# Last expert group by column halves, a one-pass second norm carried over the border, and thin norms in the second block

## The chip, the cores and the metric
The kernel runs on one core of one Trainium2 chip. The metric is the device time in microseconds from launch to end. TensorE (PE) multiplies, with its weight loads (PEld) beside it; VectorE (DVE), ScalarE (ACT) and GpSimd (POOL) work on tiles; SyncE (SP) issues the DMAs. All data is fp32.

## The reference
Two transformer blocks run one after the other, each of two layers, on 256 tokens of width 1024 (the first block adds 16 meta tokens, so T = 272 columns there). What matters here:

```
for l in range(2):                                   # first block
    mix = concat(deltanet(h), sparse_attention(h)) @ w_out[l]
    h = layer_norm(ALPHA * h + mix, ln1_g[l], ln1_b[l])
    ffn = hier_moe(h, ...)                           # 32 experts, top 2 of one group
    h = layer_norm(ALPHA * h + ffn, ln2_g[l], ln2_b[l])
layer_norm(x) = (x - mean) * rsqrt(var + 1e-5) * g + b
rms_norm(x)   = x * rsqrt(mean(x * x) + 1e-6) * g
for l in range(2):                                   # second block
    n = rms_norm(h, ln_mix[l]); mem = rms_norm(memory, mem_norm[l])
    p = n @ w_in[l]        # q, k, v, gates, ..., glow (16 columns), merge gates
    h = h + (gated sum of three branches: sparse, gated linear, memory) @ w_out[l]
    h = h + relu(rms_norm(h, ln_mlp[l]) @ w_up[l]) ** 2 @ w_down[l]
```

## The kernel before
The residual hT stays in SBUF, transposed: 8 tiles of 128 features by T tokens. A mean over features is a matmul with mean_w, a 128x128 matrix of 1/1024, summed over the eight tiles in PSUM, so each norm has 8 such products (and a layer norm 8 for the mean and 8 for the variance). In the trace one fp32 matmul leaves two records.

**Experts** (`experts`, L1409). Tokens are packed into groups of four blocks of 32 slots. For each group TensorE gathers the rows (L1401, e_sel), multiplies with w1 (L1531, x = 0) and w3 (x = 1), transposes (L1539), projects down in two banks (`down`, L1549, e_Wd), and `scatter` (L1510) spreads the result of the group before over the tokens with the gates `e_back`; VectorE adds each part to hT (L1685). Weights come over one queue, SyncE's: w1, w3 and Wd of a group are four DMAs of 1 MB each. ScalarE makes silu and copies y (L1628). A loop runs over the groups (n is read from a table); the last group follows it: turn, scatter of the group before, down, scatter of the last, its adds (L1750), and then `layer_norm_steps` (L1079): mean (L1087), subtraction (L1112), squares (L1100), variance (L1094), logarithm and exponential for the root (L1102, L1104), scale (L1115), shift (L1107). Then come the block's end, `clear` (semaphores set to zero on all engines and a barrier, L1774) and the next block of code. In layer 1 `turn_memory` (L1559) also transposes the memory tokens, ScalarE copies and squares them (L1649, L1650), and L1602 sums their squares.

**Second block** (`products`, L2118). It issues all products of w_in and w_out. Each engine's order comes from merging several streams (products, heads, sparse, gated, memory) by planned times: `F.start(key)` and `F.end(key)` come from a table of product lengths through the curve TIMES2, and the chains have fixed times. The order of products is mk (memory keys, 4), mv (memory values, 2), glow, kw, vwg (2), gqk, q and so on; two banks alternate, and ScalarE copies most results (L2292). The norm's squares are L2303, its mean square L2172, its root L2308 and L2310, its scale L2383 (`p_done`); the memory norm is L2298, L2300 and L2378. In the MLP (`mlp2`) the mean square is L3209, after the second product of 128 columns.

## Time and profile before
| | us |
|---|---|
| median of 3 runs (lowest, highest) | 2337.35 (2334.98, 2340.13) |
| the profiled execution, own time | 2336.61 |
| its span | 2334.7 |
| TensorE busy | 2144.6 |
| VectorE, ScalarE busy | 799.9, 512.2 |
| HBM read | 407.54 MB, 175 GB/s over the span |

The page gives busy time by engine; the gaps of TensorE have to be looked up in the timeline. Its stages: first block, layer 0, to 554; layer 1 to 1087; second block, branches of layer 0 to 1486 and MLP to 1713; layer 1 to the end.

### The profile page before, as it was taken

How to read it: one execution, taken by the hardware profiler on the slowest of the kernel's cores; microseconds unless marked ns; L12 is line 12 of the kernel's file. 1: busy time of each engine (PE TensorE's matmuls, PEld its weight loads, DVE VectorE, ACT ScalarE, POOL GpSimd, SP SyncE). 2: the span in 40 equal slices, each digit the busy share in tenths (PEclk: the TensorE clock that was granted, in tenths of full speed). 3: DMA queues.
4: the chain of work that ended last, by engine and by line, in shares of the span. 5: the costliest groups of instructions: out<-in, count | busy, mean ns of one | idle time of the engine just before them, and what ended most of it. 6: DMA issues, size and time to landing. Idle time of an engine off the chain costs nothing. (4 is left out here: it accounts for less than half of the span.)

```text
span 2334.7 us, 34572 instructions
## 1 busy us (share of the span) xinstructions
PE 2144.6 (92%) x13364; PEld 1646.9 (71%) x13364; DVE 799.9 (34%) x1944; ACT 512.2 (22%) x1187; POOL 64.6 (3%) x84
## 2 busy tenths in 40 slices
PE   7999989778998989778989999999999899999998
PEld 6777766445777766445757777888878577788887
DVE  3464153234465244223253323111124533221112
ACT  2313331003323431004224311100022252201000
POOL 0230000000230000000000000000000000000000
PEclk9989999999999999999999999999999999999999
DMA  6321569994321469996540434334444314343341
GB/s 219 98 91 38 228 273 386 426 424 146 122 92 38 171 276 388 424 425 226 144 153 21 161 91 129 142 144 157 166 106 144 108 67 150 109 149 139 144 144 54
DMA packets 155376, 415.22 MB, mean 178 GB/s; under 512 B 36210, under 2 KB 49756, under 8 KB 130668
## 3 DMA queue, kind: packets, MB, share of 16 engines
q1 hardware_dynamic: 155244, 413.42, 47.9%
q8 instruction: 87, 1.43, 0.2%
q14 instruction: 45, 0.37, 0.0%
HBM read 407.54 MB, written 1.05 MB: 175 GB/s over the span
## 5 line engine op out<-in xcount | busy, mean ns | idle before, releaser
L2200 PE MATMUL bank<-hT,W 128*128 128x256 f32 (+1 forms) x1440 | 328.0, 383 | 6.9 <-ACT b_gates L2350 5.9
L2200 PEld LDWEIGHTS bank<-hT,W 128*128 128x128 f32 (+1 forms) x1440 | 268.5, 190 | 53.8 <-issue 13.6
L265 PE MATMUL bank<-hT,W 128*128 128x272 f32 (+1 forms) x1056 | 262.5, 405 | 14.8 <-PEq L1774 7.6
L265 PEld LDWEIGHTS bank<-hT,W 128*128 128x128 f32 (+1 forms) x1056 | 203.0, 195 | 64.6 <-issue 18.8
L3204 PE MATMUL bank<-hT,W 128*128 128x256 f32 x1024 | 223.6, 379 | 0.0
L3220 PE MATMUL bank<-u_hid,W 128*128 128x256 f32 x1024 | 223.3, 379 | 0.0
L3204 PEld LDWEIGHTS bank<-hT,W 128*128 128x128 f32 x1024 | 194.6, 190 | 27.3 <-issue 1.0
L3220 PEld LDWEIGHTS bank<-u_hid,W 128*128 128x128 f32 x1024 | 194.6, 190 | 26.5
L1531 PE MATMUL bank<-W,e_hs 128*32 128x256 f32 x1664 | 106.9, 417 | 40.8 <-DMA W<-in_w 38.3
L1531 PEld LDWEIGHTS bank<-W,e_hs 128*32 128x32 f32 x1664 | 58.1, 120 | 91.5 <-DMA W<-in_w 44.0
L3280 DVE TENSOR_TENSOR hT<-hT,bank 128x256 f32<-128x256 f32 x128 | 53.9, 421 | 166.5 <-PE bank L3220 166.5
L3249 ACT ACTIVATE u_hid<-u_rel 128x256 f32<-128x256 f32 x64 | 26.6, 416 | 343.8 <-DVEq L3274 343.8
L1510 PE MATMUL bank<-e_back,e_y 128*128 128x272 f32 x288 | 84.5, 415 | 16.3 <-DVE hT L1685 12.2
L1401 PEld LDWEIGHTS bank<-e_sel,rowsH 128*128 128x128 f32 x768 | 92.1, 201 | 8.5 <-issue 5.3
L1401 PE MATMUL bank<-e_sel,rowsH 128*128 128x128 f32 x768 | 95.7, 287 | 1.3 <-DVEq L1729 1.3
L3272 DVE SCALAR_TENSOR_TENSOR u_rel<-bank,rstd 128x256 f32<-128x256 f32 x64 | 27.2, 425 | 203.5 <-PE bank L3204 175.9
L1510 PEld LDWEIGHTS bank<-e_back,e_y 128*128 128x128 f32 x288 | 45.6, 188 | 50.1 <-DVE hT L1685 40.3
L1549 PE MATMUL bank<-e_Wd,e_hidT 128*32 128x512 f32 x512 | 61.1, 620 | 7.7 <-DMA e_Wd<-in_w 6.6
L1194 PE MATMUL bank<-mixT,W 128*128 128x272 f32 x256 | 61.1, 393 | 2.3 <-PEq L1057 2.3
L1685 DVE TENSOR_TENSOR hT<-hT,bank 128x272 f32<-128x272 f32 x128 | 54.5, 436 | 23.3 <-PE bank L1510 19.5
L1690 DVE TENSOR_TENSOR e_hid<-e_sil,bank 128x256 f32<-128x256 f32 x16 | 9.7, 609 | 151.6 <-PE bank L1531 149.8
L1628 ACT ACTIVATE e_y<-bank 128x512 f32<-128x512 f32 x32 | 17.4, 595 | 201.4 <-PE bank L1549 187.0
(570 smaller groups left out, 2674.6 us busy)
## 6 DMA issues: line engine op xcount, KB each, us to landing
W<-in_w SPq DMA_DIRECT2D x104, 1024.0 KB, 16.7
W<-in_w_in SPq DMA_DIRECT2D x38, 2048.0 KB, 8.6
e_Wd<-in_w SPq DMA_DIRECT2D x64, 1024.0 KB, 14.2
W<-in_w_up SPq DMA_DIRECT2D x16, 2048.0 KB, 8.8
W<-in_w_down SPq DMA_DIRECT2D x16, 2048.0 KB, 7.7
e_w_ahead<-in_w SPq DMA_DIRECT2D x20, 1024.0 KB, 13.4
W<-in_w_out SPq DMA_DIRECT2D x8, 2048.0 KB, 8.2
W<-in_mem_w_kv SPq DMA_DIRECT2D x4, 2048.0 KB, 12.2
```

The costliest lines, as they stand in the source:

```text
L265: mm = nc.tensor.matmul(bank[0:rows, 0:T], w[:, k, c0:c0 + rows], m.hT[:, k, :], start=(k == 0), stop=(k == KT - 1))
L1194: mm = nc.tensor.matmul(ps[n % 4][:, 0:T], w[:, k, n % 4 * P:n % 4 * P + P], m.mixT[:, k, :], start=(k == 0), stop=(k == KT - 1))
L1401: mm = nc.tensor.matmul(o, m.rowsH[:, c, d * P:(d + 1) * P], m.sel[:, c, :], start=(c == 0), stop=(c == 2))
L1510: nc.tensor.matmul(ps[6 + d % 2][:, 0:T], y[:, d * P:(d + 1) * P], back[:, 0, :], start=True, stop=True).then_inc(S["e_part"], 1)
L1531: mm = nc.tensor.matmul(ps[2 + x][32 * j:32 * j + 32, DE * x:DE * x + DE], hs[:, k, 32 * j:32 * j + 32], weights, start=(k == 0), stop=(k ...
L1549: mm = nc.tensor.matmul(ps[4 + h][32 * j:32 * j + 32, :], hidT[:, f, 32 * j:32 * j + 32], Wd[:, j, f * D + 512 * h:f * D + 512 * h + 512], ...
L1685: nc.vector.tensor_tensor(m.hT[:, d, :], m.hT[:, d, :], ps[6 + d % 2][:, 0:T], ALU.add).then_inc(S["e_y_free"], 1)
L2200: mm = nc.tensor.matmul(o[0:n, 0:S2], w[:, k, a:a + n], m.hT[:, k, :], start=(k == 0), stop=(k == KT - 1))
L3204: mm = nc.tensor.matmul(ps[j][:, 0:S2], w[:, k, j * P:(j + 1) * P], m.hT[:, k, :], start=(k == 0), stop=(k == KT - 1))
L3220: mm = nc.tensor.matmul(ps[4 + n % 2][:, 0:S2], w[:, k, n * P:(n + 1) * P], hid[:, x, k, :], start=(k == 0), stop=(k == 3))
L3272: nc.vector.scalar_tensor_tensor(rel[:, j, :], ps[j][:, 0:S2], 0.0, m.rstd[:, :], ALU.max, ALU.mult)
L3280: nc.vector.tensor_tensor(m.xT[:, n, :], m.xT[:, n, :], ps[4 + n % 2][:, 0:S2], ALU.add).then_inc(S["u_y_free"], 1)
```

## The change
1. Experts, last group: the loop ends one group earlier. w1 of the last group, then the scatter of the group before, then w3. Wd is loaded in two halves of 512 columns, four DMAs each, on two signals. `down` is called for one half at a time; the eight last scatters use four banks and stand between and behind the halves.
2. The second layer norm is computed in one pass: the mean from the column total of hT (added up on VectorE) plus the mean of y (ScalarE's accumulator) spread by the gates; the variance from squares of the uncentred hT less the squared mean. Squares are added in pairs before the product. hT less the mean is written before the border; root, scale and shift (`norm_end`) are done behind it, in the next layer's mixers (products wait tile by tile for `n2_done`) or in the second block's start. The semaphores of the experts are cleared by GpSimd in the next mixers in layer 0, and by `clear` after layer 1.
3. Memory transpositions use two banks in turn, behind two of the norm's sums.
4. Second block and MLP: the eight squares are added on VectorE (4, 2 and 1 tiles) and one product makes the mean square, behind mk1 in both layers.
5. glow comes with vwg (168 columns instead of 152) and is transposed out of it; mv0 goes ahead of vwg, mv1 behind.

```diff
@@ projections: on_tensor, on_scalar, on_vector, on_gpsimd
                 for k in range(KT):
+                    if l and n == 0:
+                        pe.wait_ge(S["n2_done"], k + 1)
                     mm = nc.tensor.matmul(bank[0:rows, 0:T], w[:, k, c0:c0 + rows], m.hT[:, k, :], start=(k == 0), stop=(k == KT - 1))
...
+        if l:
+            yield -1.0
+            end_on_act(act)
...
+        if l:
+            yield -1.0
+            end_on_dve(dve)
+            dve.wait_ge(S["n2_done"], KT)
...
+        if l:
+            for name in EXPERTS1:
+                pool.sem_clear(S[name])
@@ new
+def norm_end(nc, m, rstd, scaled, done):
+    def on_scalar(act):
+        nc.scalar.activation(m.core.n2_rstd[:, :], m.ps[3][:, 0:T], ACT.Ln, bias=m.eps5[:, 0:1])
+        act.drain()
+        nc.scalar.activation(m.core.n2_rstd[:, :], m.core.n2_rstd[:, :], ACT.Exp, scale=-0.5).then_inc(rstd, 1)
+        for k in range(KT):
+            act.wait_ge(scaled, k + 1)
+            nc.scalar.activation(m.core.hT[:, k, :], m.core.hT[:, k, :], ACT.Identity, bias=m.core.prmT[:, 73 + k:74 + k]).then_inc(done, 1)
+    def on_vector(dve):
+        dve.wait_ge(rstd, 1)
+        for k in range(KT):
+            nc.vector.scalar_tensor_tensor(m.core.hT[:, k, :], m.core.hT[:, k, :], m.core.prmT[:, 65 + k:66 + k], m.core.n2_rstd[:, :], ALU.mult, ALU.mult).then_inc(scaled, 1)
@@ experts: SyncE
-                down(last, n + 1)
+                sp.wait_ge(S["e_down"], n + 1)
+                for h, signal in enumerate((S["e_down_in"], S["e_w3_ahead"])):
+                    for j in range(G):
+                        sp.dma_start(Wd[:, j, :].rearrange("p (f d) -> p f d", f=2)[:, :, 512 * h:512 * h + 512],
+                                     expert_weights(A, l, last[j])[2].rearrange("p (f d) -> p f d", f=2)[:, :, 512 * h:512 * h + 512]).then_inc(signal, 16)
@@ experts: TensorE
+                between(n)
+                up(n + 1, n * 64, only=(0,))
+                scatter(n + 1)
+                up(n + 1, n * 64, only=(1,))
                 turn(n + 1)
-                scatter(n + 1)
-                down(n + 1)
+                pe.wait_ge(S["n2_sums"], SUMS["total"])
+                nc.tensor.matmul(ps[2][:, 0:T], m.mean_w[:, :], total[:, 0, :], start=True, stop=False)
+                down(n + 1, halves=(0,))
+                pe.wait_ge(S["e_back"], n + 3)
+                last_scatter(0, n + 2)
+                last_scatter(1, n + 2)
+                pe.wait_ge(S["e_w3_ahead"], 64 + 64)
+                down(n + 1, halves=(1,))
+                last_scatter(2, n + 2)
+                last_scatter(3, n + 2)
+                pe.wait_ge(S["n2_sums"], SUMS["y"])
+                nc.tensor.matmul(ps[2][:, 0:T], y_mean, back[:, 0, :], start=False, stop=True).then_inc(S["n2_mean"], 1)
...
@@ experts: VectorE
+                nc.vector.tensor_tensor(total[:, :, :], m.hT[:, 0:4, :], m.hT[:, 4:8, :], ALU.add)
+                dve.drain()
+                nc.vector.tensor_tensor(total[:, 0:2, :], total[:, 0:2, :], total[:, 2:4, :], ALU.add)
+                dve.drain()
+                nc.vector.tensor_tensor(total[:, 0, :], total[:, 0, :], total[:, 1, :], ALU.add)
+                dve.drain().then_inc(S["n2_sums"], 1)
+                product(n + 1)
                 turned(n + 1)
...
+                for k in range(KT):
+                    dve.wait_ge(S["n2_squares"], k + 1)
+                    nc.vector.tensor_tensor(m.hT[:, k, :], m.hT[:, k, :], mean, ALU.subtract)
@@ Products: planned lengths
+        add(("mv", 0), 7.0, "act")
         for j in range(2):
-            add(("mv", j), 7.0, "act")
-        add("glow", 3.6, "act")
+            add(("vwg", j), 2.6, "act")
+        add(("mv", 1), 7.0, "act")
+        add("glow", 0.4, "act")
         add("kw", 3.65, "act")
-        for j in range(2):
-            add(("vwg", j), 2.4, "act")
@@ products: TensorE
-            for k in range(KT):
-                pe.wait_ge(S["p_sq"], k + 1)
-                mm = nc.tensor.matmul(ps[6][:, 0:S2], m.mean_w[:, :], m.hT[:, k, :], start=(k == 0), stop=(k == KT - 1))
-            mm.then_inc(S["p_ms"], 1)
-        if l:
-            mean_square()
+            pe.wait_ge(S["p_sum"], 1)
+            nc.tensor.matmul(ps[6][:, 0:S2], m.mean_w[:, :], m.hT[:, 0, :], start=True, stop=True).then_inc(S["p_ms"], 1)
...
+        for c in range(2):
+            mm = nc.tensor.transpose(o[0:16, c * P:(c + 1) * P], m.vwg[:, c, 152:168], m.ident[:, :])
@@ products: ScalarE, first layer
+            nc.scalar.activation(m.core.n2_rstd[:, :], m.core.n2_rstd[:, :], ACT.Exp, scale=-0.5).then_inc(S["x_rstd"], 1)
+            for k in range(KT):
+                act.wait_ge(S["x_scaled"], k + 1)
+                nc.scalar.activation(m.core.hT[:, k, :], m.core.hT[:, k, :], ACT.Identity, bias=m.core.prmT[:, 73 + k:74 + k])
+            act.drain()
+            copy(("mk", 0), m.kT[:, 0, :])
@@ products: VectorE (the MLP does the same with u_squares)
+            dve.wait_ge(S["p_sq"], KT)
+            for half in (4, 2, 1):
+                nc.vector.tensor_tensor(m.hT[:, 0:half, :], m.hT[:, 0:half, :], m.hT[:, half:2 * half, :], ALU.add)
+                dve.drain()
+            dve.drain().then_inc(S["p_sum"], 1)
```

What this makes of the order, in the words of the built programs. TensorE, end of layer 0, before (the eight single scatters L1510 of each run shown once; hT, e_y, e_back are the residual, the result, the gates):

```order
L1531 MATMUL bank<-W,e_hs 32x256 x32
...
L1539 MATMUL bank<-k_ident,e_hid 128x128 x2
...
L1510 MATMUL bank<-e_back,e_y 128x272
...
L1549 MATMUL bank<-e_Wd,e_hidT 32x512 x16
...
L1087 MATMUL bank<-hT,k_mean_w 128x272 x8
L1094 MATMUL bank<-mixT,k_mean_w 128x272 x8
L1448 UNCONDITIONAL_BRANCH
L1773 ISA x6
```

The same place in the changed program (L1549 is the scatter there, L1609 a last scatter, L1590 the down projection, L1614 a sum for the norm):

```order
L1572 MATMUL bank<-W,e_hs 32x256 x32
...
L1549 MATMUL bank<-e_back,e_y 128x272
...
L1572 MATMUL bank<-W,e_hs 32x256 x32
L1580 MATMUL bank<-k_ident,e_hid 128x128 x2
L1649 MATMUL bank<-e_w_ahead,k_mean_w 128x272
...
L1590 MATMUL bank<-e_Wd,e_hidT 32x512 x8
...
L1609 MATMUL bank<-e_back,e_y 128x272
...
L1590 MATMUL bank<-e_Wd,e_hidT 32x512 x8
...
L1614 MATMUL bank<-mixT,k_mean_w 128x272
```

The scatter of the group before stands ahead of w3, and the down projection is in two pieces with scatters between them; the 16 products of the norm are seven, among the scatters. ScalarE behind the border to layer 1, changed program:

```order
L1730 ACTIVATE mixT<-hT 128x272 x8
L1483 UNCONDITIONAL_BRANCH
L1080 UNCONDITIONAL_BRANCH
L1137 ACT_TABLE_LOAD
L1137 ACTIVATE n_rstd<-bank,eps 128x272
L1139 ACT_TABLE_LOAD
L1139 ACTIVATE n_rstd<-n_rstd 128x272
L1142 ACTIVATE hT<-hT,prmT 128x272 x8
```

Both table loads and the root stand behind the branches, that is behind the border; before, they stood ahead of it. TensorE, start of the second block, before:

```order
L2187 MATMUL bank<-b_acc,W 128x256 x16
L2172 MATMUL bank<-hT,k_mean_w 128x256 x8
L2187 MATMUL bank<-b_acc,W 128x256 x16
L2194 MATMUL bank<-W,b_acc 128x512 x8
L2800 MATMUL bank<-b_o_mem,k_mean 128x512 x2
L2194 MATMUL bank<-W,b_acc 128x512 x8
L2200 MATMUL bank<-hT,W 16x256 x8
L2200 MATMUL bank<-hT,W 128x256 x8
L2206 MATMUL bank<-W,hT 128x152 x8
```

and changed (b_acc holds the normed memory, b_vwg the product with the glow columns):

```order
L2314 MATMUL bank<-b_acc,W 128x256 x16
L2301 MATMUL bank<-hT,k_mean_w 128x256
L2314 MATMUL bank<-b_acc,W 128x256 x16
L2320 MATMUL bank<-W,b_acc 128x512 x8
L2957 MATMUL bank<-b_o_mem,k_mean 128x512 x2
L2332 MATMUL bank<-W,hT 128x168 x16
L2320 MATMUL bank<-W,b_acc 128x512 x8
L2348 MATMUL bank<-k_ident,b_vwg 16x128 x2
L2326 MATMUL bank<-hT,W 128x256 x8
```

The mean square is one product, glow two transpositions, and both vwg products stand ahead of mv1.

## Rows read from the trace of the kernel before

**Rows 1.** the page, part 1: busy time, share of the span, instructions
```profile
PE 2144.6 (92%) x13364; PEld 1646.9 (71%) x13364; DVE 799.9 (34%) x1944; ACT 512.2 (22%) x1187; POOL 64.6 (3%) x84
```

**Rows 2.** timeline, tail of layer 0: start, length (us), engine, line, operation, [idle before]
```profile
507.58 3.64 PE L1531 MATMUL bank<-W,e_hs 128*32 128x256 f32 x64
...
516.07 5.29 PE L1531 MATMUL bank<-W,e_hs 128*32 128x256 f32 x64 [4.85 <-DMA W<-in_w]
...
521.51 0.60 DVE L1690 TENSOR_TENSOR e_hid<-e_sil,bank 128x256 f32<-128x256 f32 x1 [13.36 <-PE bank L1531]
...
527.42 3.64 PE L1549 MATMUL bank<-e_Wd,e_hidT 128*32 128x512 f32 x32
...
531.22 1.08 ACT L1628 ACTIVATE e_y<-bank 128x512 f32<-128x512 f32 x2 [19.55 <-PE bank L1549]
...
532.66 5.21 PE L1510 MATMUL bank<-e_back,e_y 128*128 128x272 f32 x16 [1.60 <-ACTq L1629]
...
541.58 2.87 DVE L1112 TENSOR_TENSOR e_w_ahead<-hT,bank 128x272 f32<-128x272 f32 x8 [3.19 <-PE bank L1087]
...
548.81 3.39 DVE L1115 SCALAR_TENSOR_TENSOR e_w_ahead<-e_w_ahead,prmT 128x272 f32<-128x272 f32 x8 [4.36 <-ACT e_w_ahead L1104]
549.34 3.41 ACT L1107 ACTIVATE hT<-e_w_ahead,prmT 128x272 f32<-128x272 f32 x8 [0.57 <-DVE e_w_ahead L1115]
...
554.10 8.99 PE L265 MATMUL bank<-hT,W 128*128 128x272 f32 x32 [7.63 <-PEq L1774]
```

**Rows 3.** windows, length, busy PE, PEld, DVE, ACT, POOL; clock; DMA share; GB/s
```profile
516.00:519.00 3.00, 2.93 (x28) 1.39 (x32) 0.00 (x0) 0.00 (x0) 0.00 (x0) 0.50 1.01 426
530.00:539.00 9.00, 7.32 (x34) 3.87 (x27) 3.50 (x8) 1.08 (x2) 0.00 (x0) 1.00 1.05 387
```

**Rows 4.** the tile e_Wd, 500 to 530 us: its loads
```profile
DMA to landing us min/median/max: 10.6/13.6/16.6
```

**Rows 5.** timeline, tail of layer 1 and start of the second block
```profile
1048.78 5.17 PE L1531 MATMUL bank<-W,e_hs 128*32 128x256 f32 x64 [4.97 <-DMA W<-in_w]
...
1086.82 1.28 ACT L2298 ACT_TABLE_LOAD   x1 [1.36 <-PEq L1774]
...
1088.12 0.47 ACT L2298 ACTIVATE mem_rstd<-bank,eps 128x256 f32<-128x256 f32 x1
...
1090.41 3.26 DVE L2378 SCALAR_TENSOR_TENSOR b_acc<-xT,prmT,mem_rstd 128x256 f32<-128x256 f32 x8 [2.68 <-ACTq L2301]
1090.45 2.56 ACT L2303 ACTIVATE hT<-hT 128x256 f32<-128x256 f32 x8
...
1091.04 9.73 PE L2187 MATMUL bank<-b_acc,W 128*128 128x256 f32 x32 [3.86 <-DVE b_acc L2378]
...
1104.06 7.07 PE L2187 MATMUL bank<-b_acc,W 128*128 128x256 f32 x32
```

**Rows 6.** timeline, second block, start of its second layer
```profile
1714.95 3.72 PE L2172 MATMUL bank<-hT,k_mean_w 128*128 128x256 f32 x16 [0.18 <-ACT hT L2303]
...
1715.23 3.25 DVE L2378 SCALAR_TENSOR_TENSOR b_acc<-xT,prmT,mem_rstd 128x256 f32<-128x256 f32 x8
```

**Rows 7.** timeline, start of the first MLP
```profile
1485.75 2.56 ACT L3238 ACTIVATE u_squares<-hT 128x256 f32<-128x256 f32 x8 [43.42 <-PEq L3137]
...
1495.32 3.62 PE L3209 MATMUL bank<-u_squares,k_mean_w 128*128 128x256 f32 x16
```

**Rows 8.** timeline, second block, second layer: glow and kw, a vwg product, an addition
```profile
1747.87 7.28 PE L2200 MATMUL bank<-hT,W 128*16 128x256 f32 x32
...
1754.98 2.23 PE L2206 MATMUL bank<-W,hT 128*128 128x152 f32 x16
...
1760.45 0.69 DVE L3035 TENSOR_TENSOR b_room_g<-b_room_g 128x512 f32<-128x512 f32 x1
```

**Rows 9.** window of the second layer's branches, and its longest wait behind ScalarE
```profile
1713.00:2100.00 387.00, 366.60 (x1856) 285.55 (x1856) 136.28 (x287) 105.25 (x247) 0.00 (x0) 0.99 0.39 125
...
PE bank L2200 <- ACT b_gates L2350: 2.9, 1, 2.9
```

More of the change, by code:

```diff
@@ L1429, in experts @@
         used_up = m.w1_ahead[:, :, :].rearrange("p j n -> p (j n)")
-        m.ln_x = used_up[:, 0:KT * T].rearrange("p (k t) -> p k t", k=KT)
-        m.rstd = used_up[:, KT * T:KT * T + T]
-        m.ln_sq = m.mixT
+        total = used_up[:, 0:4 * T].rearrange("p (k t) -> p k t", k=4)
+        mean, mean_sq = [used_up[:, (4 + j) * T:(5 + j) * T] for j in range(2)]
+        y_mean = used_up[:, 6 * T:6 * T + P]
+        y_sum = used_up[:, 6 * T + P:6 * T + P + 2]
+        squares = m.mixT
         early = back[:, :, :].rearrange("p v t -> p (v t)")
@@ L1516, in up @@
                     for x, w in enumerate(("w1", "w3")):
+                        if x not in only:
+                            continue
                         if x == 0:
@@ L1540, in turn, with down @@
                     mm.then_inc(S["e_turn"], 1)
-                def down(g):
+                def down(g, halves=(0, 1)):
                     pe.wait_ge(S["e_hidT"], g + 1)
                     pe.wait_ge(S["e_down_in"], g * 64 + 64)
-                    for h in range(2):
+                    for h in halves:
                         for f in range(2):
@@ new lines, in _ @@
+                add_last(0)
+                add_last(1)
+                dve.wait_ge(S["e_y"], n + 4)
+                nc.vector.tensor_tensor(y_sum[:, 0:1], y_sum[:, 0:1], y_sum[:, 1:2], ALU.add)
+                dve.drain()
+                nc.vector.tensor_scalar(y_mean, m.ones[:, :], y_sum[:, 0:1], 1.0 / D, ALU.mult, ALU.mult)
+                dve.drain().then_inc(S["n2_sums"], 1)
+                add_last(2)
+                add_last(3)
+                add_squares(0)
+                add_last(4)
@@ L2188, in on_tensor, with memory_values @@
             mm.then_inc(S["f_mm"], 1)
-        for c in range(2):
-            yield F.start(("mv", c))
+        def memory_values(c):
             w = weights("kv1")
@@ L2207, in by_token @@
             mm.then_inc(S["f_mm"], 1)
-        yield F.start("glow")
+        yield F.start(("mv", 0))
+        memory_values(0)
         pe.wait_ge(S["p_done"], KT)
         w = weights("nkw")
-        by_feature("glow", w, 280, 16)
+        for c in range(2):
+            yield F.start(("vwg", c))
+            by_token(("vwg", c), c, w, P, 168)
+        yield F.start(("mv", 1))
+        memory_values(1)
+        yield F.start("glow")
+        pe.wait_ge(*F.made(S, ("vwg", 1)))
+        o = taken(pe, "glow")
+        for c in range(2):
+            mm = nc.tensor.transpose(o[0:16, c * P:(c + 1) * P], m.vwg[:, c, 152:168], m.ident[:, :])
+        mm.then_inc(S["f_mm"], 1)
         yield F.start("kw")
         by_feature("kw", w, 0)
-        for c in range(2):
-            yield F.start(("vwg", c))
-            by_token(("vwg", c), c, w, P, 152)
         for chunk in ("gqk", "q"):
@@ L2304, in on_scalar @@
         if l == 0:
+            copy(("mk", 1), m.kT[:, 1, :])
+        else:
             for j in range(2):
+                yield F.end(("mk", j))
                 copy(("mk", j), m.kT[:, j, :])
@@ L2311, in on_scalar @@
         act.drain().then_inc(S["p_rstd"], 1)
-        for j in range(4) if l else (2, 3):
+        for j in (2, 3):
             yield F.end(("mk", j))
             copy(("mk", j), m.kT[:, j, :])
+        yield F.end(("mv", 0))
+        copy(("mv", 0), m.mv[:, 0, :], cols=512)
         for c in range(2):
-            yield F.end(("mv", c))
-            copy(("mv", c), m.mv[:, c, :], cols=512)
+            yield F.end(("vwg", c))
+            copy(("vwg", c), m.vwg[:, c, :], cols=168)
+        yield F.end(("mv", 1))
+        copy(("mv", 1), m.mv[:, 1, :], cols=512)
         yield F.end("glow")
@@ L2322, in on_scalar @@
         copy("kw", m.raw[:, 5, :])
-        for c in range(2):
-            yield F.end(("vwg", c))
-            copy(("vwg", c), m.vwg[:, c, :], cols=152)
         for j in range(4):
@@ L3263, in _ @@
                 dve.drain().then_inc(S["u_y_free"], 2)
+                dve.wait_ge(S["u_sq"], KT)
+                for half in (4, 2, 1):
+                    nc.vector.tensor_tensor(sq[:, 0:half, :], sq[:, 0:half, :], sq[:, half:2 * half, :], ALU.add)
+                    dve.drain()
+                dve.drain().then_inc(S["u_sum"], 1)
                 dve.wait_ge(S["u_rstd"], 1)
```

150 lines of the change are left out of this document (103 added, 47 removed).

## Prediction, made before the changed kernel was run

> **What bounds the kernel now.** I read the page first. TensorE is busy for 2144.6 us of the 2334.7 us span [rows 1], so over most of the program an instruction taken from TensorE is time taken from the span, provided that nothing else becomes late. The remaining 190 us are gaps. The timeline shows where the large ones are: at the borders. From the last part of the last expert group on, TensorE waits for a chain of short steps. In layer 0 it finishes the down projection at 531.1 (527.42 + 3.64), scatters until 537.9, and then means, squares, root, scale and shift run one behind another until the next layer's first product at 554.10 [rows 2]. In layer 1 the same tail, 532.7 us later (third product group at 1048.78 against 516.07), ends in the second block's first product at 1091.04 [rows 2, 5]. The reader should see in both that every engine is idle most of the time, and that the shift on ScalarE (549.34 + 3.41 = 552.75) ends last before the border. One more wait lies ahead: the w3 product of the last group starts at 516.07 after 4.85 us of waiting for its weights [rows 2]. Between 516 and 519 the granted clock is 0.50, that is 1.2 GHz, and the 64 records take 5.29 us where the same 64 take 3.64 us at 507.58 [rows 2, 3].
>
> **A: tail of layer 0.** The scatter of the group before (8 products, 0.65 us apart, 5.2 us as in the row at 532.66) moves into the wait for w3: w1 ends at 511.2, the scatter at 516.4, just behind the landing at 516.07 [rows 2]. TensorE is then busy up to the w3 product, which I take at full clock: 3.64 us, until 520.1. VectorE gets new work there. After its adds (516.9) and the new gates (an estimate of 1.5 us) it forms the column total of the residual: 1088, 544 and 272 columns. A 512-column addition takes 0.69 us [rows 8] and one of 272 columns 0.36 us (8 in 2.87 us [rows 2]), so 1.4 + 0.7 + 0.4 and three drains give about 2.6 us, until 521.0. The gated product stands behind that in VectorE's queue: it starts at 521.0 instead of 521.51 [rows 2]. The total thus costs VectorE more than the faster w3 product leaves free, and only 0.5 us are won here. The first half of the down projection follows about 1.6 us later, at 522.6, and takes half of 3.64 us.
> The weights decide the second half. The four loads of the group land 10.6 to 16.6 us after their issue at 507.8 [rows 4], the last at about 525.8, which is 4.19 MB at 426 GB/s behind the w3 that lands at 516.0. Rows of 2 KB, which the split loads now have and which the next layer's weights have already, move at 387 GB/s [rows 3]: first half at 521.4, second at 526.8. So the first half comes in time, and the two scatters behind it (till about 526.1) too; TensorE waits 0.7 us, does the second half until 528.6, and ScalarE has copied it by 529.3. VectorE is the bound from here: the sum and mean of y (0.4), six additions with drains (3.6), three sums of squares (1.35), the copy and the squared mean (0.9), eight subtractions (2.9) and a drain, 9.3 us, so 538.6. The squares and their sums run beside that on ScalarE and TensorE. The border from 552.75 to 554.10 took 1.35 us with two barriers and the clearing [rows 2]; without the clearing I take 0.6 us: 539.2.
> Behind the border ScalarE loads a table, takes the logarithm, loads another table and takes the exponential. The same four steps take from 1086.82 to 1090.41, 3.6 us [rows 5]. The first scale and shift add 1.0 us (VectorE 548.81, ScalarE 549.34 [rows 2]). First product: 543.8 instead of 554.10, **10.3 us**. It stays between 8 (border at its old price, drains dearer) and 12 (weights half a microsecond earlier, no border).
> The table loads speak against the edit, since one of them, hidden before under the variance product, now lies on the path. In the row a load takes 1.28 us, and the logarithm follows directly [rows 5]. The sum goes by these rows. The Trainium skill ("ScalarE: Activation LUTs", section "What ACT_TABLE_LOAD costs") counts about 2.66 us for each switch, a drain included; by that page, as an estimate, each load would cost 1.4 us more. No row here shows such a drain.
>
> **B: tail of layer 1 and start of the second block.** The same walk, 532.7 us later, has the last residual square at 1068.5. Four pairs of copy and square of the memory follow on ScalarE (about 1.0 us each) until 1072.6, and the memory's mean square (3.62 us, as the like row [rows 7]) ends at 1076.3. The border with its clearing, 1.35 us, gives 1077.6 where ScalarE starts its table load at 1086.82 now. The extra logarithm costs 0.5 us, so the memory norm and mk0 start 8.7 us earlier (1082.4 for 1091.04 [rows 5]). Now comes the new wait. VectorE first does the memory norm (3.3 us from 1081.7), then eight scales (3.4 us), ScalarE the last shift, the copy of mk0 (0.9) and eight squares (2.6 us [rows 5]), VectorE three additions of 1024, 512 and 256 columns (2.6 us, priced as above): 1094.7. TensorE has done mk0 and mk1 by 1091.9 (9.5 us, part of it at the low clock, as in the row with 9.73 us against 7.07 us for the same count [rows 5]). It waits 2.8 us for the sum, spends 0.45 us on it instead of 3.45, and starts mk2 at 1095.2 instead of 1104.06: **8.9 us**. What the seven removed products save is used up by that wait. Bounds 6 and 11.
>
> **C: glow by transposition.** Two products of eight matmuls take 7.28 us for their 32 records, 3.45 us each when pipelined [rows 8]. One is removed. Two products of 152 columns (2.23 us [rows 8]) become 168 columns wide, 0.23 us more each; two transpositions and their wait I put at 0.3 us (the copy that they wait for runs under the second mv, 7 us long). 2.7 us a layer, **5.4 us**; between 4 and 6.
>
> **D: thin norms in the MLP.** 16 records in 3.62 us become 2: 3.0 us each [rows 7]. VectorE's additions are ready 2.6 us after the last square (1488.3), at 1491, and TensorE asks at 1495.32 [rows 7]; that cover is 4 us. **6.0 us**.
>
> **E: norm of the second layer of block two.** The mean square stands ahead of mk0 now (1714.95 [rows 6]); it moves behind mk1, where its sum (1721) is ready before 1722.7. mk0 starts with the memory norm, at 1715.75, 0.8 us later than TensorE starts now: 3.0 less 0.8, **2.3 us**.
>
> **F: another order in block two.** Shortening glow in the table of product times moves all later products 2.8 us earlier in the plan, and with them which product stands between two steps of the attention chains. In this stage TensorE stands still for 20.4 of 387 us a layer [rows 9], in waits of up to 2.9 us, that one of a gate product for ScalarE. Some gaps get a product in front of them (that before the gated output's mean, that before the small compression products), others lose one. I take 0; bounds -5 and +5 us a layer.
>
> **Sum.** 10.3 + 8.9 + 5.4 + 6.0 + 2.3 = 32.9 us from the profiled execution's own 2336.61 us: 2303.7. The median of the three runs is 0.7 us higher: 2304.
>
> **Rivals.** (1) The new order closes gaps, about 4 us a layer: 2296. For it speaks that two of the longer waits get a 3.45 us product ahead of them; against it, that others are uncovered. (2) The order opens gaps, some 5 us a layer: 2314. Gate products wait for ScalarE, whose queue holds whole groups of exponentials. (3) The tail of the experts does not shorten as said: if the halves of the weights do not land in order, the first half is usable only when the last transfer lands, at 526.8; scatter and second half then follow without overlap, and with the added steps on VectorE each tail gives about 4 us less: 2312. Against it: the loads of one group land spread over 6 us [rows 4]. (4) ScalarE's pipe empties at each change of tables on the new path, for as long as a load takes: two at each border, 4 x 1.28 = 5.1 us: 2309. Against it: the logarithm's row begins at 1088.12, where the load's ends [rows 5]. (It is the drain that the Trainium skill's page on ScalarE counts with each switch.) (5) Slower than before. The mechanism is the one of (2) at every gate: 24 gates a layer, each product's bank released by ScalarE behind exponentials, at the 2.9 us of the longest wait now [rows 9]. It decides from 11 added waits on (11 x 2.9 = 32); with 13 the time is 2342. Nothing but the moved order speaks for it.
> Chances: the forecast 0.55, (1) 0.17, (2) 0.12, (3) 0.09, (4) 0.05, (5) 0.02. The range takes in (1), (3) and (4), and F's bounds nearly: 2296 to 2313. A measurement of this kernel can tell about 0.2% (4.7 us) from no change; everything but (5) is beyond it: faster 0.96, same 0.02, slower 0.02.
>
> **What would show it.** In the new profile: the w3 product of the last group in about 3.7 us without a wait; the first product of layer 1 some 27.7 us behind its start (543.8 - 516.1); the mean-square product of block two as 2 records behind mk1, with a wait of about 3 us ahead of it in its first layer and none in its second; kw directly behind two short transpositions; the stage between 1713 and 2100 shorter by 5 us and by nothing else. Wrong would be: a wait of TensorE for the second half of the weights over 2 us, VectorE done with the subtractions later than 22.5 us behind the w3 product's start, or more than 26 us without work on TensorE in a layer of block two.

## The result and the profile after

Measured twice, the changed kernel has medians of 2322.75 and 2322.79 us. The second time, with six runs from 2321.34 to 2326.65 against 2336.43 us for the kernel before, the ratio is 0.9942, 95% interval 0.9926 to 0.9958. The change makes the kernel faster by 14 us, and not by 33 us: 2304 was wrong, and so was its range of 2296 to 2313.

The page of the changed kernel, part 1 (busy time, share of the span, instructions), beside [rows 1]:

```profile
PE 2124.5 (92%) x13248; PEld 1633.3 (70%) x13248; DVE 815.3 (35%) x1962; ACT 509.0 (22%) x1189; POOL 64.9 (3%) x84
```

TensorE has 20.1 us less work (2144.6 to 2124.5), and the span is 12.9 us shorter (2334.7 to 2321.8): its idle time grew from 190 to 197 us although two borders became shorter. So the question is where new idle time stands. (Busy time in these rows also grows where the granted clock is low, so part of a loss can hide in it.)

**The tail of layer 0** answers to [rows 2]. Timeline of the changed kernel: start, length, engine, line, operation, [idle before and its releaser]:

```profile
516.51 3.66 PE L1572 MATMUL bank<-W,e_hs 128*32 128x256 f32 x64 [1.32 <-DMA W<-in_w]
...
520.30 0.60 DVE L1781 TENSOR_TENSOR e_hid<-e_sil,bank 128x256 f32<-128x256 f32 x1 [0.47 <-PE bank L1572]
...
522.05 1.92 PE L1590 MATMUL bank<-e_Wd,e_hidT 128*32 128x512 f32 x16 [0.17 <-DVEq L1788]
...
527.33 1.92 PE L1590 MATMUL bank<-e_Wd,e_hidT 128*32 128x512 f32 x16 [1.11 <-DMA e_Wd<-in_w]
...
536.46 2.90 DVE L1881 TENSOR_TENSOR hT<-hT,e_w_ahead 128x272 f32<-128x272 f32 x8
...
539.69 1.28 ACT L1137 ACT_TABLE_LOAD   x1 [3.27 <-PEq L1483]
540.99 0.49 ACT L1137 ACTIVATE n_rstd<-bank,eps 128x272 f32<-128x272 f32 x1
541.53 1.28 ACT L1139 ACT_TABLE_LOAD   x1
542.82 0.43 ACT L1139 ACTIVATE n_rstd<-n_rstd 128x272 f32<-128x272 f32 x1
...
544.49 10.49 PE L267 MATMUL bank<-hT,W 128*128 128x272 f32 x32 [6.19 <-ACT hT L1142]
554.82 0.24 PE L240 MATMUL bank<-k_ident,prm 81*128 81x81 f32 x1
```

Everything stands within 1 us of where the walk had it: w3 at the full clock, though behind a wait of 1.32 us that the walk did not have, the halves in order, a wait of 1.1 us for the second one, VectorE as the bound, and the first product 27.98 us behind the w3 product. But that first group of 32 records now takes 10.49 us at a mean granted clock of 0.72, where it took 8.99 us at 0.84 [rows 2]. Other traces of the new first block give 9.0 to 10.5 us for it, and a second trace of the old one 9.43.

**Start of the second block**, beside [rows 5]:

```profile
1077.20 9.95 PE L2314 MATMUL bank<-b_acc,W 128*128 128x256 f32 x32 [4.34 <-DVE b_acc L2532]
1089.25 0.81 PE L2301 MATMUL bank<-hT,k_mean_w 128*128 128x256 f32 x2 [2.10 <-DVEq L2529]
1089.86 8.69 PE L2314 MATMUL bank<-b_acc,W 128*128 128x256 f32 x32
```

The memory's first product is 13.8 us ahead of before here (forecast: 10.3 + 8.7 = 19.0). Behind it the lead shrinks. I marked the stages by TensorE's first product in each; in us, before and after:

| stage | before | after |
|---|---|---|
| start to layer 1's first product | 554.1 | 544.5 |
| to the last expert group's w1, layer 1 | 486.1 | 489.0 |
| to the memory's first product (mk0) | 50.9 | 43.8 |
| block two, layer 0 | 394.7 | 396.9 |
| MLP 0 and start of layer 1, to its mk0 | 232.7 | 227.1 |
| block two, layer 1 | 380.9 | 388.6 |
| MLP 1 to the end | 235.2 | 232.1 |

The MLPs give their 3.0 us each, and the first one's stage also has the 2.3 us of E. The branches of block two were to become shorter and became longer in both layers. The five longest waits of TensorE in its second layer (line, releaser: us, times, longest), changed kernel, 1701.1 to 2089.7:

```profile
PE bank L2326 <- ACT b_gates L2495: 8.3, 3, 3.8
PE bank L2644 <- ACTq L2676: 3.0, 1, 3.0
PE bank L2326 <- ACT b_raw L2426: 2.6, 1, 2.6
PE bank L3114 <- DVEq L3213: 2.5, 1, 2.5
PE bank L2332 <- ACT b_mv L2426: 2.2, 1, 2.2
```

Before, the gates waited once, 2.9 us [rows 9]; now three times, 8.3 us in sum, and ahead of each a group of exponentials stands in ScalarE's queue. Here is the longest, on both engines: a gate product waits for its bank, which ScalarE frees with the tanh in the row at 2014.26, and that stands behind a group of exponentials (the first is at 2010.70) that belongs to the attention:

```profile
2010.70 0.51 ACT L2854 ACTIVATE b_room_n<-b_room_n,n_mx 128x256 f32<-128x256 f32 x1 [7.28 <-DVEq L2896]
...
2014.26 0.45 ACT L2495 ACTIVATE b_gates<-bank,b_half 128x256 f32<-128x256 f32 x1
...
2005.68 3.62 PE L2326 MATMUL bank<-hT,W 128*128 128x256 f32 x16
...
2014.86 5.31 PE L2326 MATMUL bank<-hT,W 128*128 128x256 f32 x16 [3.84 <-ACT b_gates L2495]
```

The product whose bank the tanh frees was done at 2009.30 (2005.68 + 3.62). ScalarE had no work then: it stood idle for 7.28 us, until VectorE gave it what the exponentials need at 2010.70. So it is the place of the tanh in the queue that makes TensorE wait, and not the load of ScalarE.

The gate product behind the wait takes 5.31 us, at a mean granted clock of 0.69, for the same 16 records that take 3.62 at 2005.68. The wait costs its own 3.8 us and 1.7 us of low clock. The one long gate wait of the kernel before had the same price behind it:

```profile
2024.49 5.38 PE L2200 MATMUL bank<-hT,W 128*128 128x256 f32 x16 [2.95 <-ACT b_gates L2350]
```

The fifth wait is another new one. ScalarE copies mv0 only behind the memory keys' norm, and the second vwg needs that bank:

```profile
1728.34 1.06 ACT L3001 ACTIVATE b_o_mem<-b_o_mem 128x1024 f32<-128x1024 f32 x1
1729.49 0.60 ACT L2426 ACTIVATE b_mv<-bank 128x512 f32<-128x512 f32 x1
...
1725.52 2.44 PE L2332 MATMUL bank<-W,hT 128*128 128x168 f32 x16
1730.14 3.65 PE L2332 MATMUL bank<-W,hT 128*128 128x168 f32 x16 [2.18 <-ACT b_mv L2426]
1733.59 7.65 PE L2320 MATMUL bank<-W,b_acc 128*128 128x512 f32 x16
```

Before, the second mv product, 7 us long, ran over that copy.

### The profile page after: what moved, and what is told of

Read it like the earlier page. It is cut to its first block and busy times, and to the rows that moved or that the text cites. A ratio compares the mean times of both kernels' runs of the same rounds, so it can differ in the third digit from the quotient of the medians.

```text
span 2321.8 us, 34408 instructions
## 1 busy us (share of the span) xinstructions
PE 2124.5 (92%) x13248; PEld 1633.3 (70%) x13248; DVE 815.3 (35%) x1962; ACT 509.0 (22%) x1189; POOL 64.9 (3%) x84
## 5 line engine op out<-in xcount | busy, mean ns | idle before, releaser
L2326 PE MATMUL bank<-hT,W 128*128 128x256 f32 x1408 | 331.3, 392 | 22.8 <-ACT b_gates L2495 16.6
L2326 PEld LDWEIGHTS bank<-hT,W 128*128 128x128 f32 x1408 | 272.1, 196 | 69.2 <-issue 29.3
L267 PEld LDWEIGHTS bank<-hT,W 128*128 128x128 f32 (+1 forms) x1056 | 205.3, 197 | 63.8 <-issue 16.7
L3361 PE MATMUL bank<-hT,W 128*128 128x256 f32 x1024 | 223.6, 379 | 0.0
L3361 PEld LDWEIGHTS bank<-hT,W 128*128 128x128 f32 x1024 | 194.6, 190 | 27.3 <-issue 1.0
L1549 PE MATMUL bank<-e_back,e_y 128*128 128x272 f32 x256 | 74.4, 413 | 14.3 <-DVE hT L1776 11.9
L1590 PE MATMUL bank<-e_Wd,e_hidT 128*32 128x512 f32 x512 | 64.4, 644 | 9.7 <-DMA e_Wd<-in_w 8.3
L1549 PEld LDWEIGHTS bank<-e_back,e_y 128*128 128x128 f32 x256 | 40.6, 188 | 43.6 <-DVE hT L1776 40.3
L1226 PEld LDWEIGHTS bank<-mixT,W 128*128 128x128 f32 x256 | 48.5, 190 | 12.6 <-issue 2.8
L2420 PE MATMUL bank<-b_acc,W 128*128 128x256 f32 x256 | 55.6, 379 | 0.0
```

Of the source, the lines that this page charges most:

```text
L267: mm = nc.tensor.matmul(bank[0:rows, 0:T], w[:, k, c0:c0 + rows], m.hT[:, k, :], start=(k == 0), stop=(k == KT - 1))
L1226: mm = nc.tensor.matmul(ps[n % 4][:, 0:T], w[:, k, n % 4 * P:n % 4 * P + P], m.mixT[:, k, :], start=(k == 0), stop=(k == KT - 1))
L1549: nc.tensor.matmul(ps[6 + d % 2][:, 0:T], y[:, d * P:(d + 1) * P], back[:, 0, :], start=True, stop=True).then_inc(S["e_part"], 1)
L1590: mm = nc.tensor.matmul(ps[4 + h][32 * j:32 * j + 32, :], hidT[:, f, 32 * j:32 * j + 32], Wd[:, j, f * D + 512 * h:f * D + 512 * h + 512], ...
L2326: mm = nc.tensor.matmul(o[0:n, 0:S2], w[:, k, a:a + n], m.hT[:, k, :], start=(k == 0), stop=(k == KT - 1))
L2420: mm = nc.tensor.matmul(o[:, 0:S2], w[:, k, n % 4 * P:n % 4 * P + P], m.acc[:, k, :], start=(k == 0), stop=(k == KT - 1))
```

## The experiments

Two theories stood against each other at first. M: the moved order in block two takes back what the thinner products give. N: the first block's part fell short, and block two gave what was forecast. K is a third: the low granted clock behind the shorter gaps is the loss. Every ratio is to the kernel before, run beside the kernel named.

**The parts apart.** The first kernel puts block two and the MLPs back as they were, with glow as a product, the long mean squares and the old table of product times. Against the changed kernel, its core:

```
-            pe.wait_ge(S["p_sum"], 1)
-            nc.tensor.matmul(ps[6][:, 0:S2], m.mean_w[:, :], m.hT[:, 0, :], start=True, stop=True).then_inc(S["p_ms"], 1)
+            for k in range(KT):
+                pe.wait_ge(S["p_sq"], k + 1)
+                mm = nc.tensor.matmul(ps[6][:, 0:S2], m.mean_w[:, :], m.hT[:, k, :], start=(k == 0), stop=(k == KT - 1))
+            mm.then_inc(S["p_ms"], 1)
...
-        add("glow", 0.4, "act")
+        add("glow", 3.6, "act")
...
+        by_feature("glow", w, 280, 16)
```

> Only the first block's part of the change (tail of the last expert group, one-pass norm over the border); the second block and both MLPs keep the products, the norms and the order of before. Theory M (the moved order of block two eats what its thinner products give): the trace of the changed kernel is 13.8 us ahead at the second block's first product, the long mean square costs about 1 us against the sum's wait, and nothing is lost behind that: 2336.2 - 13 = 2323, the same time as the whole change. Rival N (the first block's part fell short and the second block gave the 13.7 us forecast): this kernel then stands at 2323 + 13.7 = 2336, no faster than before.

Measured: 2322.79 us, ratio 0.9938 (0.9923 to 0.9954), the time of the whole change. N falls. All that the other parts were to bring, 13.7 us and more, is lost within block two. In its trace the second layer of block two takes 380.8 us (before 380.9).

The next one adds the thin norms alone and leaves glow and the order as before; of the diff above it has the lines from `add("glow"` on:

> The first block's part of the change and the thin norms of block two and of the MLPs; glow stays a product of its own, and the order on TensorE is that of before. Theory M: the thin norms give what was forecast for them, 3.0 us in each MLP, 2.3 us in the second layer of block two and 0.7 us in its first: 2322.8 - 9 = 2313.8. Rival (the thin norms give nothing, VectorE's additions being late): 2322.8.

Measured: 2315.1 us, ratio 0.9904 (0.9882 to 0.9926), 7.7 us below the first. The thin norms are worth about what was said, by the medians; the runs spread from 2310 to 2323 us, and the interval just touches that of the first kernel. What is left, glow by transposition with the order that comes with it, makes the kernel 7.7 us *slower* again.

**The order.** On the changed kernel, the planned lengths alone:

```
-        add("kw", 3.65, "act")
+        add("kw", 6.45, "act")
```

> The whole change, but in the table of product times kw has 6.45 us instead of 3.65, so that every product behind kw keeps the place in the plan that it had before; no instruction is added or removed. Theory M: the 15 us that block two lost (5.1 and 9.9 in its two layers) come back but for the wait on the copy of the first mv product, 2.2 us a layer: 2322.7 - 10.6 = 2312. Rival (the loss is that wait and the low clock behind it alone, or scattered clock drops with no cause in the order): 2320 to 2323.

Measured: 2318.65 us, ratio 0.9924 (0.9906 to 0.9942). That is 4 of the 10.6 us that M said, between M and the rival, and the runs scatter (2313.5 to 2325.3), so this kernel alone decides nothing. In its trace the waits for the gates are back at 2.9 us and those for L2644, b_raw of mq and L3114 are gone, but kw's copy waits 1.6 us a layer, since ScalarE now has the decay gate's exponential ahead of it.

The same with mv's second product ahead of vwg again (in the table, and in TensorE's and ScalarE's code likewise):

```
         for j in range(2):
+            add(("mv", j), 7.0, "act")
+        for j in range(2):
             add(("vwg", j), 2.6, "act")
-        add(("mv", 1), 7.0, "act")
```

> As the kernel with kw at 6.45 us, and the second mv product goes back ahead of the two vwg products, so that ScalarE's copy of the first mv has 7 us of product over it again; the transpositions then wait for the second vwg's copy, about 0.9 us. Behind kw the order on TensorE is that of before. Theory M: the wait of 2.2 us a layer goes, 0.9 us comes: 2.6 us in all below the kernel with kw at 6.45 us alone, about 2309. If the copy's wait had only hidden another (the scaled input or nkw's weights), no gain over that kernel.

Measured: 2309.11 us, ratio 0.9891 (0.987 to 0.9911). The time is M's, but the step from the kernel with kw at 6.45 us is 9.5 us where 2.6 was expected; the two traces differ by only 1.0 us in block two and by 4.0 us ahead of it, where the programs are the same. Such a step between two kernels with scattered runs (this one has four runs near 2308 and two near 2318) is not to be read as the price of one edit.

The order by itself, on the kernel before:

```
-        add("glow", 3.6, "act")
+        add("glow", 0.8, "act")
```

> The kernel of before with one number changed: glow has 0.8 us instead of 3.6 in the table of product times. No instruction is added, removed or shortened; behind kw the order on TensorE is word for word that of the changed kernel. Theory M: the order alone costs about 10 us in the two layers of block two (2322.7 - 2309.1 = 13.6, less some 3.5 for the wait on the copy of the first mv): 2338.1 + 10 = 2348. Rival (the moved order costs nothing by itself, only together with the shorter products): 2338.

Measured: 2342.45 us (twelve runs), ratio 1.002 (1.0008 to 1.0032): 4.2 us slower by the medians, between 2 and 7.5 by the interval. No instruction was changed. Its longest waits in block two are those of the changed kernel to the tenth (gates 8.3 in 3, then 3.0, 2.6 and 2.5). The sign is M's, the size is less than half of the 10 us expected.

**All together.** Two more moves on the kernel with mv and the plan put back:

```
-            if j == 2:
+            if j == 3:
                 mean_square()
...
-        add("kw", 6.45, "act")
+        add("kw", 6.0, "act")
         for j in range(4):
-            add(("gqk", j), 3.65, "act")
+            add(("gqk", j), 3.65 if j else 4.1, "act")
```

> The kernel with the second mv ahead of vwg and the later products at their old places, and two more moves: the mean square of block two goes behind mk2 instead of mk1 (ScalarE copies mk2 ahead of the root), and 0.45 us of the planned length goes from kw to the product behind it, so that ScalarE copies kw ahead of the decay gate's exponential. In the trace of the kernel without them TensorE waits 3.3 us for the sum in the first layer of block two and 1.6 us a layer for kw's copy. Theory M (each wait comes straight off the time): 2309.1 - 3.3 - 3.2 = 2302.6. Rival (the waits are hidden behind others): 2307 to 2309.

Measured: 2305.98 us, ratio 0.9864 (0.9841 to 0.9886), 32 us below the kernel before: faster than both kernels, and with the least scatter so far (2303.6 to 2306.4). The waits for the sum and for kw's copy are gone from its trace; of the 6.5 us expected for them the medians show 3.1.

To price each part from this quiet end, four kernels ran on one chip: this one, this one with mv as in the change, this one with the planned times as in the change, and the change itself. The second and the third, against the first:

```
+        add(("mv", 0), 7.0, "act")
         for j in range(2):
-            add(("mv", j), 7.0, "act")
-        for j in range(2):
             add(("vwg", j), 2.6, "act")
+        add(("mv", 1), 7.0, "act")
```

```
-        add("kw", 6.0, "act")
+        add("kw", 3.65, "act")
         for j in range(4):
-            add(("gqk", j), 3.65 if j else 4.1, "act")
+            add(("gqk", j), 3.65, "act")
```

> The kernel with the three moves once more, as the near end of the ledger on the same chip: 2306 us, with the kernels beside it read against it.

> The kernel with the three moves (label e6_three), but with the second mv product behind the two vwg products again, as in the changed kernel; everything behind kw stays at its old place. Theory M: the second vwg waits 2.2 us for ScalarE's copy of the first mv, kw 0.5 us, and the transpositions' 0.4 us goes: 2 x 2.3 = 4.6 us over the kernel with the three moves. Theory K (the gap also drops the granted clock, as in one layer of the changed kernel, where the second vwg took 3.65 us instead of 2.55): up to 8 us over it. Rival (only scattered runs made the difference between the two kernels run before): no more than 1 us over it.

> The kernel with the three moves, but with kw and the product behind it at 3.65 us in the table, so that all later products stand where the changed kernel has them; the order of mv, vwg and of the mean square stays. Theory M: the moved order costs what it cost alone on the kernel before, about 4.5 us, and 3.2 us more for kw's copy, which stands behind the decay gate's exponential again: 6 to 8 us over the kernel with the three moves. Rival (order costs nothing once the waits at the stage's start are gone): the same time.

> The changed kernel itself, on the same chip as the kernels beside it, as the far end of the ledger. If the parts add up (mv's place, the later products' places, the wait for the sum of 2.1 to 3.5 us in the first layer), it stands 13 to 17 us over the kernel with the three moves; if parts hide behind each other, it stands closer to the larger of them, 8 us over it.

| kernel | median, us | over the first |
|---|---|---|
| three moves | 2305.07 | 0 |
| mv as in the change | 2307.55 | 2.5 |
| later products' places as in the change | 2316.76 | 11.7 |
| the changed kernel | 2322.79 | 17.7 |

The places of the later products are the large part. The expectation was 6 to 8 us, and one of its reasons was wrong: the b_raw wait in that order is for a copy of mq (at 1866.76 in the second layer), not for kw's. mv's place costs 2.5 us by the median, where 4.6 was expected, with two of six runs some 9 us higher; the rest is 3.5 us, of which the wait for the sum explains 2.1. The ratios of the second and third to the kernel before, 0.9885 (0.9863 to 0.9908) and 0.9911 (0.9895 to 0.9928), overlap, so the split between them is less sure than their order. Block two's branches take 390.1 and 390.8 us in the two layers with the moved places, 385.3 and 383.6 without. The longest waits of TensorE in the second layer, first with the moved places, 1692.6 to 2083.5:

```profile
PE bank L2326 <- ACT b_gates L2497: 8.3, 3, 3.8
PE bank L2646 <- ACTq L2678: 3.0, 1, 3.0
PE bank L2326 <- ACT b_raw L2426: 2.6, 1, 2.6
PE bank L3116 <- DVEq L3215: 2.5, 1, 2.5
PE bank L2990 <- DVE b_room_g L3058: 2.1, 4, 0.5
```

and with three moves, 1687.5 to 2071.1:

```profile
PE bank L2990 <- DVE b_room_g L3058: 3.6, 7, 0.5
PE bank L2326 <- ACT b_gates L2497: 2.9, 1, 2.9
PE bank L119 <- DVE b_room_n L2545: 2.3, 1, 2.3
PE bank L3116 <- DVE b_room_g L3220: 2.3, 3, 0.9
PE bank L2659 <- DVEq L2744: 2.2, 1, 2.2
PE bank L3142 <- ACTq L3173: 1.6, 1, 1.6
```

All waits of that stage sum to 21.1 and 18.1 us, besides the 1.1 us for the memory's norm that both have at its start: 3.0 us a layer. The first layer has the same difference, so the added waits come to 6 us in two layers. The windows of the two second layers show the rest (length, busy time, clock near the end; with the moved places first):

```profile
1692.65:2083.46 390.81, 368.88 (x1825) 289.02 (x1825) 136.51 (x284) 102.55 (x242) 0.00 (x0) 0.96 0.38 124
```

```profile
1687.50:2071.10 383.60, 364.43 (x1825) 284.23 (x1825) 136.53 (x284) 103.36 (x242) 0.00 (x0) 0.98 0.39 126
```

The same 1825 records keep TensorE busy 4.4 us longer, at a mean granted clock of 0.96 for 0.98; in the first layer it is 2.2 us. So about half of the 12 us by which these stages of the two traces differ is waits, and the rest is the clock. Three waits with the product behind them, from the kernel with the moved places:

```profile
1926.38 3.69 PE L2326 MATMUL bank<-hT,W 128*128 128x256 f32 x16 [1.01 <-ACT b_gates L2497]
...
1961.91 5.32 PE L2326 MATMUL bank<-hT,W 128*128 128x256 f32 x16 [3.44 <-ACT b_gates L2497]
...
2007.47 6.41 PE L2326 MATMUL bank<-hT,W 128*128 128x256 f32 x16 [3.84 <-ACT b_gates L2497]
```

Behind 1 us of waiting the product has its usual length; behind 3.4 and 3.8 us it is 1.6 and 2.7 us longer (mean granted clock 0.69 and 0.57 in it).

**The clock.** Products of 128x512 into free banks (results overwritten) fill the gaps of the changed kernel: six ahead of layer 1's first product (shown), four ahead of the memory's first product and two ahead of the sum:

```
+            if l and n == 0:
+                spare_products(nc, bank, m.ident[:, :], w[:, 0, 0:512], 6)
```

> The whole change, with products into free banks while TensorE waits: 6 of 128x512 ahead of layer 1's first product, 4 ahead of the memory's first product, 2 ahead of the mean square of block two's first layer. Their results are overwritten. Theory K (the low granted clock behind the shorter borders costs time): the first product group behind the border takes 7.5 us instead of 10.5, and 3 us come back in layer 1, perhaps 1 to 2 more behind the second border: 2318 to 2320. Rival: the clock behind the border stays as it is, or TensorE is late by the added products: 2323 or more.

Measured: 2322.64 us, ratio 0.9936 (0.9921 to 0.9951). The rows at the two gaps:

```profile
543.61 5.39 PE L119 MATMUL bank<-W,k_ident 128*128 128x512 f32 x12 [1.43 <-PEq L1485]
548.84 7.50 PE L269 MATMUL bank<-hT,W 128*128 128x272 f32 x32
...
1078.14 7.17 PE L2320 MATMUL bank<-b_acc,W 128*128 128x256 f32 x32 [0.78 <-DVE b_acc L2538]
1085.15 1.88 PE L119 MATMUL bank<-W,k_ident 128*128 128x512 f32 x4
1090.27 1.22 PE L2305 MATMUL bank<-hT,k_mean_w 128*128 128x256 f32 x2 [3.24 <-DVEq L2535]
```

The clock does what theory K says: 7.50 us for 10.49, 7.17 for 9.95. The total does not move. At the second gap one reason is in the rows: TensorE is sooner at the sum and waits 3.24 us instead of 2.10. At the first gap the rows show a gain: from the first table load of the border (543.57 here, 539.69 without the added products) to the end of the first group it is 12.8 us for 15.3, although the added products hold the first product up by 0.5 us. What takes it back in this trace stands ahead of the first added product, where no instruction differs: w3 starts at 518.98, and the second half of the down projection takes 3.37 us for 1.92, at a mean granted clock of 0.55. With the sum asked for later, and 5 and 4 such products, the same was tried on the kernel with three moves:

```
+                spare_products(nc, bank, m.ident[:, :], w[:, 0, 0:512], 5)
...
+                spare_products(nc, o, m.ident[:, :], w[:, 0, 0:512], 4)
```

> As the kernel before it, with products into free banks while TensorE waits: 5 of 128x512 ahead of layer 1's first product, 4 ahead of the memory's first product. Theory K (clock): layer 1's first products take 7.5 us instead of 10.1 to 10.5, mk0 and mk1 7.2 instead of 8.8 to 10; the second gain was given back to the wait for the sum before, and is kept now that the sum is asked for later. 2.5 and 2 us below the kernel without them: 2298. Rival (the clock is lost again in the next gap, or the sum's wait takes it): no gain over that kernel.

Measured: 2306.85 us, ratio 0.9859 (0.9836 to 0.9883), runs from 2297.3 to 2308.9, against 2305.98 us without them. The first group takes 7.60 us, mk0 and mk1 7.17, and nothing is left of it in the median. This trace, too, is late ahead of the added products: w3 starts at 519.24 and the second half takes 3.52 us, while w3 starts between 515.8 and 518.2 in the ten traces of the new first block without added products, of which two have such a slow second half. So filling these gaps brought nothing in the median, but the two runs do not show that the low clock behind them costs nothing; why the stretch ahead of them is late is open.

The Trainium skill ("TensorE: Matmul & The Clock Gate", section "HAM oscillation — how this bites in real kernels") prices time at the low clock at half its length. For the product behind a gap the trace agrees: 5.31 us at a mean granted clock of 0.69 give, as an estimate, 0.31 x 5.31 = 1.6 us, and it is 1.7 us longer than the product at 2005.68. The sum over the program did not follow that price in these two kernels.

## Why the prediction was wrong, step by step

- **A, the tail of layer 0 (10.3 us).** Right in mechanism and near in size. From the w3 product to the first product 27.98 us for 27.7 forecast; the wait for the second half 1.11 us for 0.7; the subtractions end 22.85 us behind w3's start (539.36 less 516.51), 0.35 us over the limit I had set. The lead at the first product was 9.6 us. What the step missed is the product behind the gap: 1.5 us of the lead is lost to it in this trace; over ten traces the group takes 9.9 us on the mean, for 9.2 in two traces of the old first block. Nor is the full clock in the tail sure: in the trace with the moved places w3 waits 2.13 us and takes 5.35.
- **The layer behind it.** I counted nothing for it. From layer 1's first product to the last expert group, two traces of programs with the old first block take 486.1 and 484.7 us, ten with the new one without added products 485.9 to 489.4, mean 488.1. That is 2.7 us more, of which the point above is a part. The clock goes with it: one minus the granted clock, summed over the stage, is 22.5 us on the mean for 19.6. One place in the changed kernel's trace, where the like product took 3.93 us before:

```profile
662.87 5.62 PE L267 MATMUL bank<-hT,W 128*128 128x272 f32 x16
```

  Why the clock falls there is open: the last wait ahead of it is 0.99 us where it was 0.81.
- **B, the tail of layer 1 (8.9 us).** From the last w1 to mk0 43.8 us for 50.9; mk0 to mk2 12.66 us for 12.8 forecast. By its own steps 7.5 us; over all traces the stage to mk0 went from 51.7 to 43.4, 8.3 us. With A and B alone the kernel gained 15.3 us by the medians, for 19.2 less 0.7 forecast.
- **D and E (8.3 us).** Right within the scatter: 7.7 us measured for 9.0 with the sum's 0.7 us. The mean square in the MLP is one short row, with no wait:

```profile
1483.66 0.59 PE L3365 MATMUL bank<-u_squares,k_mean_w 128*128 128x256 f32 x2
```

- **C, glow by transposition (5.4 us).** Right as the price of the products, as far as the medians tell: with the places and mv put back it takes the kernel with thin norms from 2315.1 to 2309.1, 6.0 us, with intervals that overlap. Wrong as it stands in the change. I wrote that "the copy that they wait for runs under the second mv" and looked only at the transpositions' wait. The second vwg's bank is that of mv0 as well, and its copy stands behind the memory keys' norm on ScalarE. I had the rows for that in the trace of before and did not follow the bank. Cost: 2.2 us of wait a layer, 2.5 us in the median.
- **F, another order in block two (0, bounds -5 to +5 a layer).** This is the step that failed: a term put at 0. It is 11.7 us in two layers against the kernel with three moves, just outside the bounds (10 us for two layers); by itself, on the kernel before, it is 4.2 us, inside them. I had taken the middle. I had the new order in hand and averaged over it as if gaps opened and closed by chance. What opened is visible in it: at three gates ScalarE's queue now has a group of exponentials ahead of the tanh, where one gate had it before. The waits it opened are 1.0 to 3.8 us long, and the longer ones bring low clock with them; those it closed were 0.2 to 2.3 us. In sum it adds 3.0 us of waits a layer, the same on both kernels; what the clock adds differs.
- **The rivals.** (2), the order opens gaps, was the right one, at 5.9 us a layer for the 5 it named, of which 3.0 are waits; its 2314 lacks the clock behind the first border, mv's copy and the part of A and B that fell short. (1) and (5), an order that gains or one that outweighs everything, did not come. (3) and (4) did not happen either: the halves land in order, and the function starts where the table load ends (539.69 + 1.28, then 540.99). The drain that the Trainium skill counts with each switch ("ScalarE: Activation LUTs", section "What ACT_TABLE_LOAD costs") does not show here.
- **The signs.** Those of the borders came: the sum is asked for by 2 records behind mk1, with a wait of 2.10 us in the first layer and none in the second. The second layer's branches, which were to become 5 us shorter, became 5.0 us longer (389.9 for 384.9 us from that layer's first product to the MLP's). Of the three signs of being wrong two came: VectorE was done 22.85 us behind w3's start, and TensorE had no work for 26.3 us (396.91 less 370.62) in block two's first layer, against the limit of 26:

```profile
1077.20:1474.11 396.91, 370.62 (x1825) 289.37 (x1825) 139.88 (x292) 106.97 (x254) 0.00 (x0) 0.96 0.39 125
```

The shortfall of 19 us (32.9 less 13.6) is thus, in order of size: the places of the later products (11.7), A, B and the layer between them (about 3), mv's place (2.5); the rest, about 2, is not assigned and lies within the scatter of the medians. That the order alone costs 4.2 us on the kernel before and 11.7 us on the kernel with three moves, with the same 6 us of added waits, stays open; the mean granted clock over the runs, 0.970 in both of the first pair and 0.968 for 0.972 in the second, says that the difference is in the clock, not why.

## What to carry to other kernels

Where a table of planned times sets the order, a shortened product moves all that comes behind it: keep the plan's total when you change a length, and judge the moved order by itself, with the lengths of before. For each product that now comes sooner, follow its bank to the copy that frees it, and that copy to what stands ahead of it in its engine's queue. Price a long wait on TensorE higher than its length: behind 3.4 and 3.8 us the next product was 1.6 and 2.7 us longer. Before you call a filled gap useless, see where the time went that it won. Price two small edits from the variant whose runs scatter least.

## What the hardware showed that was not expected

The waits that the order of block two sets are the same from trace to trace to a tenth of a us, and the clock is not. Behind the same wait of 2.99 us the same six records take 2.84 us in the changed kernel, at a granted clock of 1.00 (first row), and 5.49 us in the one with three moves and the moved places, at 0.50 (second):

```profile
1808.10 2.84 PE L2644 MATMUL bank<-b_room_n,k_mean 128*128 128x512 f32 x6 [2.99 <-ACTq L2676]
```

```profile
1795.26 5.49 PE L2646 MATMUL bank<-b_room_n,k_mean 128*128 128x512 f32 x6 [2.99 <-ACTq L2678]
```

The kernel before ran from 2331.1 to 2344.7 us on one chip, with its mean granted clock between 0.973 and 0.966. Filling gaps raised the clock behind them (10.49 to 7.50 us) and left the median where it was, twice.
